# Two-layer trunk on one core: layers unrolled without barriers, a five-slot weight ring that keeps the low half in place, a new beginning, and weights split in halves of a tile

## The chip, the core and the metric

The kernel runs on one core of one Trainium2 chip. The metric is device time in microseconds (us), the lower the better. Five engines run their own instruction streams, tied together by semaphores only: PE (matmuls), DVE (vector), ACT (scalar, activations), POOL (GpSimd) and SP (SyncE, which here only issues DMAs and waits).

## The reference, cut to what matters

D = 1024, SEQ = 1024, batch 1, two layers, all float32:

```python
c_act = silu(c)
for l in range(2):
    sh_a, sc_a, ga_a, sh_m, sc_m, ga_m = split(c_act @ w_ada[l] + b_ada[l], 6)
    h = rmsnorm(x, g_mix[l]) * (1 + sc_a) + sh_a
    z = h @ w_in[l] + b_in[l]
    cb, cc, cu, q, kc, vc, ks, vs, kw, vw, nsa_g, merge_g = split(z)
    y_conv = short_conv(cb, cc, cu, conv_w[l]) @ w_up_conv[l]
    y_attn = nsa(rope(q), rope(kc), vc, rope(ks), vs, rope(kw), vw, nsa_g) @ w_up_attn[l]
    x = x + ga_a * ((sigmoid(g_c) * y_conv + sigmoid(g_a) * y_attn) @ w_o[l])
    h = rmsnorm(x, g_mlp[l]) * (1 + sc_m) + sh_m
    x = x + ga_m * (square(relu(h @ w_ff1[l])) @ w_ff2[l])
return rmsnorm(x, g_final)
```

`nsa` compresses kc and vc by a small MLP over blocks of 32 tokens and attends over the compressed blocks, over 8 selected blocks of 64 tokens, and over a window of 512.

## The kernel before, in words

**Layout.** Activations stand transposed in SBUF: `xT` is 8 chunks of 128 channels x 1024 tokens. A f32 product is three matmuls: both operands are split into a high part, rounded by writing it as fp32r (`hH`, `whi`), and a low part, the rest (`hL`, `wlo`); PE adds high·high, low·high and high·low (`dense`, L737 to L761). A weight tile is 128x1024 words (512 KB) and gives 8 x 3 products, each as a pair of matmuls of 512 columns: 48 matmuls.

**Weights.** `weight_plan` (L73) writes one layer's list of tiles: `split` (dense weights), `ada` (128 columns of `w_ada`, all 1024 rows) and `cmp` (a quarter of a compression weight). The first 32 dense tiles have an `ada` tile of this layer behind each, the first 16 `w_ff1` tiles one of the next layer (of layer 0's in the last layer, where nothing uses it). All go through a ring `wraw` of RAW = 3 slots in the list's order: SP (L670 to L698) loads tile n once the one three before it has let go, a `split` tile by `w_split` (POOL has split it), an `ada` tile by `ada_used` (DVE), a `cmp` tile by `cmp_used` (PE reads it directly, L813). POOL (L701 to L733) splits whole tiles into two slots of `whi` and `wlo`, L730 rounding and L732 subtracting, and waits there for the slot's last matmul (`lin_done`); PE waits for `w_split` once a tile. `ada_products` (L384) is a multiply of 1024 columns and a reduction on DVE, `ada_column` (L395) a matmul with a column of ones.

**Stages of a layer,** in PE's order: norm; conv branch (`cc`, `cu`, `cb` by 4); `gc`, `gc`, `uc` by 4 (a `uc` tile serves two short products); `ga`; `kc`, `vc`, `q0` to `q2`, compression of k, `q3`, compression of v, `ks`, `vs`, `kw`, `nsa`, `vw`, attention, `ua`, `wo`; norm; MLP (`f1`, `f2`). A norm: PE sums squares by 32 matmuls of one column (L406), DVE (L1283) and ACT make the reciprocal root, PE spreads it over `aux`, DVE multiplies chunk k (L1316), ACT writes `hH` (L1030), DVE `hL` (L1307). PE takes `cc0` and `cu0` side by side, chunk by chunk as `hL` comes.

**The beginning** (L410 to L579), a block of its own: DVE makes the rope tables, the x tiles are transposed (L506) as DVE works, ACT copies and squares, and DVE goes through the 16 `ada` tiles that the first norm needs, all through the ring of three. Then a block end, `clear()`, and the loop: `nc.Fori(0, DEPTH)` (L667) around one block, with `clear()` (L630) after each layer, where each engine clears a fifth of the semaphores between barriers. SP's first DMAs in a layer are three tiles, then `x_keep` (L680, all of `xT` to DRAM for the residual, 4 MB); DVE and ACT wait for it ahead of the conv branch, whose buffers lie over `xT`.

**The end** (L1644 to L1692): g_final on DVE and ACT, transposes back, outputs scaled and stored by token tile.

## Time and profile before

| | |
|---|---|
| three runs | 3528.22, 3532.52 (median), 3535.51 us |
| profiled execution: its own time, its span | 3531.86, 3530.1 us |
| PE busy, share of the span | 94% |
| DVE, POOL, ACT busy | 52%, 32%, 22% |
| DMA | 256.92 MB, mean 73 GB/s |

The span runs from the first to the last instruction; 1.8 us of the execution's time lie around it. PE is busy nearly throughout, so the time is PE's work plus the stretches in which it waits: these are read from the windows and from PE's waits by place. A matmul's "idle before" says how long PE stood still and which instruction released it.

### The profile page before, as it was taken

To read this page: it belongs to the slowest core of one execution; us is meant where nothing else is said; L and a number is where in the kernel's file an instruction comes from. 1 tells how busy PE (TensorE), PEld (TensorE's weight loads), DVE (VectorE), ACT (ScalarE), POOL (GpSimd) and SP (SyncE) were. 2 spreads that over 40 slices of the span, in tenths; PEclk is the share of its full clock that TensorE was granted. 3 is DMA by queue.
4 is the path that set the end of the run, shared out by engine and by line. 5 is a ranking of instruction groups with operands and counts; after the bars stand their busy time and mean duration, and the time that the engine had idled before them with its cause. 6 is when DMAs were issued, how large, how long until landed. Compare 5 with 4: busy or idle time off the path is not lost. (4 is left out here: it accounts for less than half of the span.)

```text
span 3530.1 us, 39234 instructions
## 1 busy us (share of the span) xinstructions
PE 3308.0 (94%) x15575; PEld 2687.7 (76%) x15605; DVE 1830.5 (52%) x1877; ACT 781.0 (22%) x1283; POOL 1119.9 (32%) x800
## 2 busy tenths in 40 slices
PE   4999999898898999999979999989979899999998
PEld 3788887676687888888868888767658788888887
DVE  7754344787636444333365443568865564433333
ACT  2100012666312000000120001147661210000002
POOL 3333322233332333333323333222333233333331
PEclk6999999999899999999989999999999999999999
DMA  5434431000422222111133343300005132211111
GB/s 166 147 96 131 138 96 48 1 1 1 157 66 66 72 72 68 52 48 48 36 122 96 113 137 111 81 7 1 1 9 195 37 96 72 72 48 48 48 48 60
DMA packets 349011, 256.92 MB, mean 73 GB/s; under 512 B 9500, under 2 KB 335506, under 8 KB 348563
## 3 DMA queue, kind: packets, MB, share of 16 engines
q1 hardware_dynamic: 334642, 209.75, 20.3%
q10 hardware_dynamic: 14177, 44.56, 3.4%
q8 instruction: 126, 2.06, 0.2%
q14 instruction: 66, 0.54, 0.0%
HBM read 223.87 MB, written 30.41 MB: 72 GB/s over the span
## 5 line engine op out<-in xcount | busy, mean ns | idle before, releaser
L730 POOL TENSOR_SCALAR whi<-wraw 128x1024 fp32r<-128x1024 f32 x238 | 266.2, 1119 | 1848.7 <-PE lin L759 1246.0
L759 PE MATMUL lin<-hH,whi 128*128 128x512 f32 x2272 | 719.1, 398 | 43.5 <-POOL wlo L732 35.4
L759 PE MATMUL lin<-hL,whi 128*128 128x512 f32 x2272 | 705.8, 392 | 0.0
L759 PE MATMUL lin<-hH,wlo 128*128 128x512 f32 x2272 | 705.2, 392 | 0.0
L732 POOL TENSOR_TENSOR wlo<-wraw,whi 128x1024 fp32r<-128x1024 f32 x238 | 644.2, 2707 | 19.9
L759 PEld LDWEIGHTS lin<-hH,whi 128*128 128x128 f32 x2272 | 423.9, 190 | 136.5 <-POOL wlo L732 39.5
L759 PEld LDWEIGHTS lin<-hL,whi 128*128 128x128 f32 x2272 | 430.5, 189 | 90.9
L759 PEld LDWEIGHTS lin<-hH,wlo 128*128 128x128 f32 x2272 | 429.9, 189 | 90.1
L1600 DVE SCALAR_TENSOR_TENSOR xT<-lin,adac,xT 128x1024 f32<-128x1024 f32 x144 | 184.8, 1283 | 542.3 <-PE lin L759 541.9
L711 POOL TENSOR_SCALAR prob<-prob,fac 128x640 f32<-128x640 f32 (+7 forms) x256 | 182.6, 713 | 471.2 <-DVE fac L1528 453.3
L759 PE MATMUL lin<-hidH,whi 128*128 128x512 f32 x1024 | 316.0, 390 | 0.0
L759 PE MATMUL lin<-hidL,whi 128*128 128x512 f32 x1024 | 315.5, 389 | 0.0
L759 PE MATMUL lin<-hidH,wlo 128*128 128x512 f32 x1024 | 315.5, 389 | 0.0
L1238 ACT ACTIVATE tmp<-lin 128x1024 f32<-128x1024 f32 x64 | 65.8, 1028 | 1077.6 <-PE lin L759 1076.5
L393 DVE TENSOR_REDUCE adared<-wraw 128x128 f32<-128x1024 f32 x112 | 223.3, 1993 | 94.8 <-PE pv L398 91.7
L1620 DVE TENSOR_TENSOR tmp<-tmp 128x1024 f32<-128x1024 f32 x64 | 84.0, 1313 | 352.0 <-ACT tmp L1238 352.0
L1544 DVE TENSOR_TENSOR pTL<-aux,pTH 128x512 fp32r<-128x512 f32 (+8 forms) x296 | 198.3, 686 | 50.9 <-ACT pTH L1188 49.4
L759 PEld LDWEIGHTS lin<-hidL,whi 128*128 128x128 f32 x1024 | 192.3, 188 | 39.9
L759 PEld LDWEIGHTS lin<-hidH,wlo 128*128 128x128 f32 x1024 | 192.3, 188 | 39.8
L759 PEld LDWEIGHTS lin<-hidH,whi 128*128 128x128 f32 x1024 | 191.8, 188 | 39.4
L388 DVE TENSOR_TENSOR wraw<-wraw,cT 128x1024 f32<-128x1024 f32 x112 | 201.2, 1796 | 27.3 <-DMA wraw<-in_w_ada 26.4
L1538 DVE TENSOR_REDUCE negm<-lin 128x1 f32<-128x640 f32 (+7 forms) x256 | 177.6, 703 | 37.3 <-PE lin L935 35.8
(233 smaller groups left out, 4025.5 us busy)
## 6 DMA issues: line engine op xcount, KB each, us to landing
wraw<-in_w_ff SPq DMA_DIRECT2D x128, 512.0 KB, 3.9
wraw<-in_w_ada SPq DMA_DIRECT2D x112, 512.0 KB, 4.8
wraw<-in_w_in SPq DMA_DIRECT2D x78, 512.0 KB, 3.8
x_keep<-xT SPq DMA_DIRECT2D x2, 4096.0 KB, 16.0
mix_keep<-tmp ACTq DMA_DIRECT2D x16, 512.0 KB, 2.6
gate_keep<-ropes ACTq DMA_DIRECT2D x16, 512.0 KB, 2.8
stG<-gate_keep ACTq DMA_DIRECT2D x16, 512.0 KB, 4.2
stM<-mix_keep ACTq DMA_DIRECT2D x16, 512.0 KB, 5.5
```

What stands on the lines that cost most here:

```text
L388: dve.tensor_tensor(w, w, cT[:, :].rearrange("p (k o) -> p k o", o=1).to_broadcast([P, KC, P]), ALU.mult).then_inc(ada_prod, 1)
L393: dve.tensor_reduce(adared[:, no % 2, :], w.rearrange("p k n -> p n k"), AX.X, ALU.add).then_inc(ada_used, 1)
L711: pool.tensor_scalar(p, p, fac[:, st["no"] % 2, i:i + 1], 1.0, ALU.mult, ALU.mult).then_inc(p_scaled, 1)
L730: pool.tensor_scalar(whi[:, s % SPL, :], wraw[:, n % RAW, :], 1.0, 1.0, ALU.mult, ALU.mult).then_inc(w_hi, 1)
L732: pool.tensor_tensor(wlo[:, s % SPL, :], wraw[:, n % RAW, :], whi[:, s % SPL, :].bitcast(F32), ALU.subtract).then_inc(w_split, 1)
L759: mm = pe.matmul(lin[c % 2][:, hf], w, m(k)[:, hf], start=first, stop=last)
L1238: act.activation(tmp[:, 0, :], slot(("f1", f))[:, :], ACT.Relu).then_inc(relu_made, 1)
L1538: dve.tensor_reduce(negm[:, m:m + 1], scores(u)[:, at:at + st["n"]], AX.X, ALU.max, negate=True).then_inc(max_made, 1)
L1544: dve.tensor_tensor(pt("low", x, r), turned(x, r), pt("high", x, r).bitcast(F32), ALU.subtract).then_inc(t_free[x["bank"]], 1)
L1600: dve.scalar_tensor_tensor(out=xT[:, i, :], in0=slot(name)[:, :], scalar=adac[:, gate + i:gate + i + 1], in1=xT[:, i, :], op0=ALU.mult, op ...
L1620: dve.tensor_tensor(tmp[:, 1, :], tmp[:, 0, :], tmp[:, 0, :], ALU.mult).then_inc(hid_sq, 1)
```

## The change

What it does:

- **No loop and no barriers.** The body is now `layer_programs(layer)` (after, L772), called for both layers; each engine runs beginning, layer 0, layer 1 and end in one block. `clear()` is gone; semaphores count on, or each layer has its own. A layer's first norm sums squares like the others.
- **Ring.** RAW = 5 slots. `wlo` is now `wraw` itself: POOL writes the low part over the raw tile, `whi` keeps its own two slots. A `split` tile's ring slot so comes free only with its last matmul (`lin_done`), and SP waits for that. Five slots of 4 KB and two of `whi` take the room of the former three and four (28 KB a partition both).
- **Halves.** POOL rounds and subtracts 512 columns at a time, with one `w_split` for each; PE waits ahead of k = 0 and of the middle k.
- **`w_ada` by rows.** A tile is 4 k-rows x 256 columns; DVE multiplies each row by its scalar of `cT` and adds, 4 instructions of 256 columns; two tiles make two column blocks. The 16 tiles that the last layer loaded for no use are gone.
- **Beginning.** x is transposed token tile by token tile and copied by DVE; ACT squares the token rows and sums them (`accum_out`); w_ada's first 2048 columns come as 16 DMAs of 512 KB with 2 KB runs, half 0 over `r_h` beside `xin`, half 1 in `r_m`; the norm's first four chunks wait for half 0 alone. The rope tables are made after `cb0`, in the conv branch. `x_keep` is two DMAs of 2 MB from ACT's queue. Layer 0's waits as before: ACT for its second half at the head of the conv branch (L1168), DVE as well (L1411).
- Next layer's `x_keep` is issued by ACT behind its squares (L1396); PE transposes the next layer's parameters in the sixth group of `f1` (L1146).

The diff's core:

```diff
-RAW = 3
+RAW = 5
...
-        (whi, wlo), (prob3,) = region("r_w", 2 * SPL * 1024, [(n, [P, SPL, 1024], F32R) for n in ("whi", "wlo")],
-                                      [("prob3", [P, HPG, SEQ], F32)])
+        (whi, wraw), (_, wlo), (prob3, pTH3, pTL3) = region(
+            "r_w", (SPL + RAW) * 1024,
+            [("whi", [P, SPL, 1024], F32R), ("wraw", [P, RAW, 1024], F32)],
+            [("whi_", [P, SPL, 1024], F32R), ("wlo", [P, RAW, 1024], F32R)],
...
 SP:
-                        if n >= RAW:
-                            o = n - RAW
-                            sp.wait_ge(dict(split=w_split, ada=ada_used, cmp=cmp_used)[TILES[o][0]], KIND_NO[o] + 1)
+                    if o is not None:
+                        if TILES[o][0] == "split":
+                            sp.wait_ge(lin_done, CHUNK[TILES[o][1], TILES[o][6][-1]] + 1)
+                        else:
+                            sp.wait_ge(dict(ada=ada_used, cmp=cmp_used)[TILES[o][0]], KIND_NO[o] + 1)
...
 POOL:
-                        pool.tensor_scalar(whi[:, s % SPL, :], wraw[:, n % RAW, :], 1.0, 1.0, ALU.mult, ALU.mult).then_inc(w_hi, 1)
-                        pool.wait_ge(w_hi, s + 1)
-                        pool.tensor_tensor(wlo[:, s % SPL, :], wraw[:, n % RAW, :], whi[:, s % SPL, :].bitcast(F32),
-                                           ALU.subtract).then_inc(w_split, 1)
+                    for i, hf in enumerate(half):
+                        raw, high = wraw[:, SLOT[n], hf], whi[:, s % SPL, hf]
+                        pool.tensor_scalar(high, raw, 1.0, 1.0, ALU.mult, ALU.mult).then_inc(w_hi, 1)
+                        pool.wait_ge(w_hi, 2 * s + i + 1)
+                        pool.tensor_tensor(wlo[:, SLOT[n], hf], raw, high.bitcast(F32), ALU.subtract).then_inc(w_split, 1)
...
 PE, dense:
-                            if j == 0:
-                                pe.wait_ge(w_split, SPLIT_NO[n] + 1)
+                            if j == 0 and k % (kk // 2) == 0:
+                                pe.wait_ge(w_split, 2 * s + k // (kk // 2) + 1)
...
 DVE, ada_products:
-            dve.tensor_tensor(w, w, cT[:, :].rearrange("p (k o) -> p k o", o=1).to_broadcast([P, KC, P]),
-                              ALU.mult).then_inc(ada_prod, 1)
-            dve.tensor_reduce(adared[:, no % 2, :], w.rearrange("p k n -> p n k"), AX.X, ALU.add).then_inc(ada_used, 1)
+            for i in range(ADA_K):
+                c = cT[:, ADA_K * t[3] + i:ADA_K * t[3] + i + 1]
+                if t[3] == 0 and i == 0:
+                    ins = dve.tensor_scalar(total, w[:, i, :], c, None, ALU.mult)
+                else:
+                    ins = dve.scalar_tensor_tensor(out=total, in0=w[:, i, :], scalar=c, in1=total, op0=ALU.mult, op1=ALU.add)
...
 begin_vector, after the copies of x:
+            ada(0, 0)
+            norm_diag(dve, 0)
+            for k in range(1, KC):
+                ada(0, k)
+            modulation(0)
+            dve.wait_ge(spread, 2)
+            norm_scaled(dve, 0, 0)
+            for k in range(1, 4):
+                norm_scaled(dve, 0, k)
+                norm_low(dve, 0, k - 1)
+                ada(1, k - 1)
+            norm_low(dve, 0, 3)
+            for k in range(3, KC):
+                ada(1, k)
+            modulation(1)
...
-            clear()
...
 scalar, head of a layer:
+                if layer:
+                    norm_root(act, n0)
...
+                else:
+                    keep_x(act, 0)
+                act.wait_ge(x_out[1], 16)
```

**POOL, one weight tile** (`lin_done` is PE's release of the slot, `raw_in` the tile's arrival, `w_hi` and `w_split` POOL's own steps). Before:

```order
L730 TENSOR_SCALAR whi<-wraw 128x1024 [waits lin_done,raw_in1,w_split]
L732 TENSOR_TENSOR wlo<-wraw,whi 128x1024 [waits w_hi]
```

and of the change:

```order
L867 TENSOR_SCALAR whi<-wraw 128x512 [waits lin_done,raw_in4,w_split]
L869 TENSOR_TENSOR wlo<-wraw,whi 128x512 [waits w_hi]
L867 TENSOR_SCALAR whi<-wraw 128x512
L869 TENSOR_TENSOR wlo<-wraw,whi 128x512 [waits w_hi]
```

Two instructions of 1024 columns become four of 512, in the order round, subtract, round, subtract, and the ring slot is written where it was read.

**SP, around the compression**, from the load of `q3` to that of `ks` (an ISA row at L698 is a wait carried by itself ahead of the DMA below it). Before:

```order
L698 ISA [waits cmp_used]
L698 DMA wraw<-in_w_in 128x8x128
L693 DMA wraw<-in_cmp_v_w 64x4x256 [waits cmp_used]
L693 DMA wraw<-in_cmp_v_w 64x4x256
L693 DMA wraw<-in_cmp_v_w 64x4x256 [waits cmp_used]
L693 DMA wraw<-in_cmp_v_w 64x4x256
L693 DMA wraw<-in_cmp_v_w 64x4x256 [waits w_split]
L693 DMA wraw<-in_cmp_v_w 64x4x256
L693 DMA wraw<-in_cmp_v_w 64x4x256 [waits cmp_used]
L693 DMA wraw<-in_cmp_v_w 64x4x256
L698 ISA [waits cmp_used]
L698 DMA wraw<-in_w_in 128x8x128
```

and of the change:

```order
L430 DMA wraw<-in_w_in 128x8x128 [waits lin_done]
L423 DMA wraw<-in_cmp_v_w 64x4x256 [waits cmp_used]
L423 DMA wraw<-in_cmp_v_w 64x4x256
L423 DMA wraw<-in_cmp_v_w 64x4x256 [waits cmp_used]
L423 DMA wraw<-in_cmp_v_w 64x4x256
L423 DMA wraw<-in_cmp_v_w 64x4x256 [waits cmp_used]
L423 DMA wraw<-in_cmp_v_w 64x4x256
L423 DMA wraw<-in_cmp_v_w 64x4x256 [waits cmp_used]
L423 DMA wraw<-in_cmp_v_w 64x4x256
L430 DMA wraw<-in_w_in 128x8x128 [waits lin_done]
L430 DMA wraw<-in_w_in 128x8x128 [waits cmp_used] x4
```

The first and the last-but-one load, `q3` and `ks`, now wait for `lin_done`, the end of an earlier tile's matmuls, and the eight loads of `cmp_v` stand behind the first of them.

**DVE, the beginning**, from the rope tables to the first `ada` tiles before (`adared`, `wraw`):

```order
L569 SCALAR_TENSOR_TENSOR nf<-nf 128x1024 [waits dve_p] x4
L572 TENSOR_SCALAR nf<-nf 128x1024 [waits dve_p]
L575 TENSOR_SCALAR nt<-nf 128x1024 [waits p_act]
L388 TENSOR_TENSOR wraw<-wraw,cT 128x1024 [waits raw_in0]
L393 TENSOR_REDUCE adared<-wraw 128x128 [waits ada_prod]
L388 TENSOR_TENSOR wraw<-wraw,cT 128x1024 [waits raw_in1]
```

and of the change, from the diagonal of the norm on (`acc` holds the sums over rows, `nt` a scaled chunk, `hL` its low part):

```order
L513 TENSOR_TENSOR tmp<-ident,rms 128x512
L715 SCALAR_TENSOR_TENSOR acc<-adar,cT,acc 128x1024 [waits adar0_in0]
L715 SCALAR_TENSOR_TENSOR acc<-adar,cT,acc 128x1024 [waits adar0_in1,dve_step] x2
L715 SCALAR_TENSOR_TENSOR acc<-adar,cT,acc 128x1024 [waits adar0_in2,dve_step] x2
L715 SCALAR_TENSOR_TENSOR acc<-adar,cT,acc 128x1024 [waits adar0_in3,dve_step] x2
L484 TENSOR_TENSOR adac<-pv,cols 128x4 [waits p_col]
L484 TENSOR_TENSOR adac<-pv,cols 128x4 [waits dve_step]
L489 SCALAR_TENSOR_TENSOR modA<-adac,cols 128x4 [waits dve_step]
L521 SCALAR_TENSOR_TENSOR nt<-xT,modA,aux 128x1024 [waits spread,p_vec]
L521 SCALAR_TENSOR_TENSOR nt<-xT,modA,aux 128x1024
L526 SCALAR_TENSOR_TENSOR hL<-nt,adac,hH 128x1024 [waits h_hi]
L713 TENSOR_SCALAR acc<-adar,cT 128x1024 [waits adar1_in0]
```

The rope work is no longer ahead of `w_ada`, the multiply and reduction of each column tile are one multiply-add for each k-row, and the first chunks' normalization stands ahead of the second half's sums.

## Rows read from the trace of the kernel before

**Rows 1.** The page, part 1: busy us, share of the span, instructions of each engine.

```profile
PE 3308.0 (94%) x15575; PEld 2687.7 (76%) x15605; DVE 1830.5 (52%) x1877; ACT 781.0 (22%) x1283; POOL 1119.9 (32%) x800
```

**Rows 2.** Table of stretches: length, busy us by engine (instructions), granted clock, DMA.

```profile
0.00:96.50 96.50, 38.94 (x141) 30.03 (x141) 71.83 (x58) 27.66 (x35) 34.50 (x72) 0.63 0.58 187
...
1106.50:1786.20 679.70, 679.65 (x3005) 563.33 (x3006) 279.50 (x162) 70.28 (x68) 239.77 (x122) 1.00 0.19 58
```

**Rows 3.** Timeline of the beginning: start, us, engine, line, operation, [idle before <-releaser].

```profile
14.34 3.67 PE L506 MATMUL lin<-ident,xin 128*128 128x128 f32 x16 [1.74 <-DMA xin<-in_x]
...
16.73 5.71 DVE L569 SCALAR_TENSOR_TENSOR nf<-nf 128x1024 f32<-128x1024 f32 x4
...
61.60 6.97 PE L406 MATMUL aux<-ones,tmp 128*128 128x1 f32 x32
...
96.49 1.19 PE L759 MATMUL lin<-hH,whi 128*128 128x512 f32 x2 [6.42 <-POOL wlo L732]
...
101.21 1.28 DVE L1307 SCALAR_TENSOR_TENSOR hL<-nt,adac,hH 128x1024 fp32r<-128x1024 f32 x1
...
101.33 1.15 ACT L1030 ACTIVATE hH<-nt,adac 128x1024 fp32r<-128x1024 f32 x1 [1.36 <-DVE nt L1316]
...
122.59 0.72 PE L759 MATMUL lin<-hH,whi 128*128 128x512 f32 x2 [2.24 <-POOL wlo L732]
```

**Rows 4.** DMA view of the first 20 us: GB/s in 40 slices of 0.5 us.

```profile
GB/s 0 0 0 8 8 172 238 377 418 442 393 385 410 393 426 434 393 434 410 418 442 385 401 411 403 411 339 329 304 285 298 293 297 286 291 292 290 159 19 0
```

**Rows 5.** The page, part 6: DMA issues, KB each, median us to landing.

```profile
wraw<-in_w_in SPq DMA_DIRECT2D x78, 512.0 KB, 3.8
x_keep<-xT SPq DMA_DIRECT2D x2, 4096.0 KB, 16.0
```

**Rows 6.** Stretches from the last pair before a norm to the next stage's first pair.

```profile
1064.35:1078.27 13.92, 7.57 (x38) 4.82 (x36) 6.82 (x9) 4.83 (x5) 3.39 (x2) 0.69 0.00 0
1786.44:1811.93 25.49, 9.16 (x39) 6.11 (x37) 10.99 (x15) 5.97 (x6) 7.62 (x4) 0.56 0.52 185
```

**Rows 7.** Timeline: the norm's first DVE instruction before the MLP and before layer 1.

```profile
1069.04 0.17 DVE L1283 TENSOR_SCALAR rms<-aux 128x8 f32<-128x8 f32 x1 [3.13 <-PE aux L406]
...
1798.60 0.17 DVE L1283 TENSOR_SCALAR rms<-aux 128x8 f32<-128x8 f32 x1 [10.28 <-issue]
```

**Rows 8.** Waits of PE from 110 to 500 us, then from 1815 to 2220 us.

```profile
PE lin L759 <- POOL wlo L732: 6.2, 5, 2.2
...
PE lin L759 <- POOL wlo L732: 6.5, 5, 2.2
```

**Rows 9.** Timeline: first pair of the third `w_ff1` tile, layers 0 and 1.

```profile
1106.55 0.79 PE L759 MATMUL lin<-hH,whi 128*128 128x512 f32 x2 [3.84 <-POOL wlo L732]
...
2821.90 1.22 PE L759 MATMUL lin<-hH,whi 128*128 128x512 f32 x2 [5.07 <-POOL wlo L732]
```

**Rows 10.** POOL by form: TENSOR_SCALAR of 512 columns (busy us, mean ns | idle before).

```profile
L711 POOL TENSOR_SCALAR prob<-prob,fac 128x512 f32<-128x512 f32 x32 | 22.6, 708 | 48.8 <-DVE fac L1528 46.5
```

**Rows 11.** Timeline, POOL's subtraction with DVE idle, and beside DVE's adds of two tensors.

```profile
88.94 2.34 POOL L732 TENSOR_TENSOR wlo<-wraw,whi 128x1024 fp32r<-128x1024 f32 x1
...
520.55 9.56 DVE L1415 TENSOR_TENSOR blk<-vcT,pe_cols 64x1008 f32<-64x1008 f32 x4
...
520.84 3.82 POOL L732 TENSOR_TENSOR wlo<-wraw,whi 128x1024 fp32r<-128x1024 f32 x1
```

**Rows 12.** Timeline: last quarter of the first compression, and the rotation behind `q3`.

```profile
517.72 2.05 PE L813 MATMUL pv<-blk,wraw 128*128 128x126 f32 x16 [2.01 <-DMA wraw<-in_cmp_k_w]
...
553.96 1.88 PE L790 MATMUL aux<-fbuf,rot 128*128 128x512 f32 x4
```

**Rows 13.** Line 398, matmuls: duration ns min/median/max.

```profile
L398 PE MATMUL pv<-ones,adared x224: 167/250/374, 30.1 to 3121.7; 128*128 128x1 f32 x112
```

**Rows 14.** Timeline of the end: last sum of squares, first scaled output.

```profile
3505.44 2.51 PE L406 MATMUL aux<-ones,tmp 128*128 128x1 f32 x16 [0.86 <-ACT tmp L1223]
...
3515.49 0.75 DVE L1684 TENSOR_SCALAR outb<-lin,rms 128x512 f32<-128x512 f32 x1
```

More of the change, by code:

```diff
@@ L76, in weight_plan @@
     tiles, chunk = [], {}
-    ada = iter(range(ADA_FIRST, NADA))
-    def dense(src, row, col, names, with_ada=False):
-        for n in names:
-            chunk[n] = len(chunk)
-        tiles.append(("split", src, row, col, 8 // len(names), names))
-        if with_ada:
-            tiles.append(("ada", next(ada)))
-    for j in range(CONV_W // P):
-        for name, off in (("cc", O_CC), ("cu", O_CU), ("cb", O_CB)):
-            dense("w_in", 0, off + P * j, [(name, j)], True)
-    for i in range(0, KC, 2):
-        dense("w_in", 0, O_MG + P * i, [("gc", i)], True)
-        dense("w_in", 0, O_MG + P * (i + 1), [("gc", i + 1)], True)
-        dense("w_up_conv", 0, P * i, [("uc", i), ("uc", i + 1)], True)
@@ L400, in sum_squares, with ada_column @@
+        def ada_column(pe, g, group):
+            pe.wait_ge(ada_used, ADA_TILES * (group + 1))
+            for i in range(2):
+                at = ADA_W // P * g + i
+                mm = pe.matmul(pv[:, 0, at:at + 1], adared[:, group % 2, i * P:(i + 1) * P], ones[:, 0:1], start=True, stop=True)
+            mm.then_inc(ada_mm, 1)
         def sum_squares(pe, first, last):
@@ new lines, in norm, with squares @@
+        def norm(dve, n, ready):
+            dve.wait_ge(ss_done, n)
+            dve.tensor_scalar(rms[:, :], aux[:, 0:NT], 1.0 / D, EPS, ALU.mult, ALU.add).then_inc(mean_made, 1)
+            norm_diag(dve, n)
+            ready()
+            dve.wait_ge(spread, 2 * (n + 1))
+            for k in range(KC):
+                norm_scaled(dve, n, k)
+                if k:
+                    norm_low(dve, n, k - 1)
+            norm_low(dve, n, KC - 1)
+        def squares(act, i, n, made):
+            act.wait_ge(x_made, made + i + 1)
+            if i >= 2:
+                act.wait_ge(ss_added, (n - 1) * (KC - 2) + i - 1)
+            act.activation(tmp[:, min(i, 1), :], xT[:, i, :], ACT.Square).then_inc(sq_made, 1)
@@ new lines, in scalar @@
+                if layer:
+                    fetch_tables()
+                for j in range(CONV_W // P):
+                    if j:
+                        freed(act, ("cu", j - 1))
+                    done(act, ("cc", j))
+                    act.activation(fbuf[:, 0, :], slot(("cc", j))[:, :], ACT.Identity,
+                                   bias=col(R_BIN + O_CC // P + j)).then_inc(free_sem(("cc", j)), 1)
+                    act.wait_ge(conv_made, v0 + j + 1)
+                    act.activation(cvH[:, j, :], ropes[:, 1, :], ACT.Copy).then_inc(cv_hi, 1)
+                    if layer == 0 and j == 0:
+                        rope_scalar(act)
+                    if layer == 0 and j == 1:
+                        act.wait_ge(rope_out, 32)
+                        fetch_tables()
@@ new lines, in vector @@
+                    done(dve, ("uc", i))
+                    if i >= 2:
+                        dve.wait_ge(mix_out[i % 2], 16 * (i // 2))
+                    dve.tensor_tensor(tmp[:, i % 2, :], slot(("uc", i))[:, :], fbuf[:, i % 2, :], ALU.mult).then_inc(free_sem(("uc", i)), 1)
+                    if i % 2:
+                        ada()
+                for i in range(KC):
+                    ada()
+                dve.wait_ge(ada_mm, layer * N_ADA + N_ADA - ADA_FIRST)
+                ada_part(dve, ADA_W // P * ADA_FIRST, NADA)
```

2286 lines of the change are left out of this document (1169 added, 1117 removed).

## The prediction

> **What bounds the kernel.** I read, in this order, the page's busy times, a table of stretches, PE's waits, and the timeline at the places where PE waits. PE is busy 3308.0 of 3530.1 us [rows 1]; from the MLP's third tile on it works 679.65 of 679.70 us at full clock [rows 2]. The change adds no matmul there, so it can win only where PE stands still. In the first 96.5 us PE does 38.94 us of work, none of it a dense product; `cb0`, behind the two products that wait for the norm, begins at 122.59 [rows 3]. The layer boundary takes 25.49 us where the same norm ahead of the MLP takes 13.92 [rows 6]. PE waits for POOL's split in the conv and `uc` stage, 6.2 us in layer 0 and 6.5 in layer 1 [rows 8], and at the third `w_ff1` tile, 3.84 and 5.07 us [rows 9]. The sum is made against the profiled execution, 3531.86 us; the median of the runs is 0.7 above that.
>
> **Beginning: −38 us.** Compared is the start of `cb0`, before 122.59 [rows 3]. The new chain, as times from the start:
> - x (4 MB) lands by about 13, at some 400 GB/s in the slices of [rows 4], and can be transposed from its first quarter on, near 7. 64 transposes at 3.67/16 = 0.23 us make 14.7 us, 8 copies on DVE at about 1.28 each less; so the copies are done at about 22 (20 to 25).
> - DVE then needs the parameters 1, `ada(0,0)` and the diagonal 2.3, seven multiply-adds of 1024 columns at 5.71/4 = 1.43 [rows 3], 10, columns and modulation 3 to 4, then two scaled chunks and a low part at 1.28: the first `hL` at 43. Three more chunks with a multiply-add of half 1 between take 4.0 each, five more multiply-adds 7, columns and modulation 4.5, and the last chunks 2.5 each, since ACT's 1.15 lies beside them: the eighth `hL` at about 75.
> - The data are no bound: by 400 GB/s half 0 of `w_ada` (4 MB) has landed near 24 and half 1 near 38.
> - PE does 6 pairs for each chunk of `cc0` and `cu0` beside that, and ends near 82: 2.7 us of the last chunk, and some backlog from chunks worked off at the low clock, at which a pair takes 1.19 in place of 0.79 or 0.72 [rows 3]; the positions' matmuls add 2.
> - `x_keep` is the other term. ACT issues it after its last `hH`, near 74; 4 MB took 16.0 us [rows 5], so the 2 MB that ACT and DVE wait for take about 8.5, and ACT drains `cc0` at about 83 to 84.
>
> So `cb0` starts at about 84.5, 38 us sooner; 30 to 41 by the ends above. The rope tables, ten DVE operations of 1.3 to 1.4 us, go beside the next two products, some 21 us, with 0 to 3 us to spare; ACT's sine work beside them too.
>
> **Boundary: −10.** Without block end, `clear()` and fetching the first tiles anew, the norm should look like the one ahead of the MLP: DVE's first instruction waits 3.13 us there, 10.28 here, with no releaser but issue [rows 7]. 25.49 − 13.92 = 11.6, less about 1.6 for the two `x_keep` issues and the root's table on ACT. Ends: 0 and −12.
>
> **Stalls in the mixed stages: −16.** Two tiles follow each other with little PE work between them (a `uc` product is half as long), and PE waits for load and split. With five slots the load is earlier, and the first half is ready after half a rounding, 0.71 [rows 10], and half a subtraction, 1.2 to 1.9 by 2.34 alone and 3.82 beside DVE [rows 11]: 2.0 in place of 3.5 to 4.9 us. Of 6.2 + 6.5 I take off 9.7, of 3.84 + 5.07 6.4. Ends: −10 and −19.
>
> **Compression and `ks`: +3.** Layer 0 waits 2.01 us for a quarter of `cmp_k` [rows 12], and nearly as long for one of `cmp_v`; with five slots both go, −4. In layer 1 the load of `q3` waits for the end of `q2`, and `cmp_v` stands behind it in SP's queue: nothing won. The load of `ks` now waits for `q3`'s last matmul, since the low half holds the slot: 3.8 landing [rows 5] and 2.0 for the first half, less the rotation's 1.88 [rows 12] and what is left: 3.5 us of new wait a layer, +7. Ends: −4 and +15.
>
> **The edits with one answer.** 16 fewer ada columns at 250 ns [rows 13], −4. The wait for each half inside a tile: 0, since POOL's four instructions take 4.0 to 4.6 us in all and PE's tile 10.9 (48 matmuls, 24 pairs at .45); they end long before PE comes to the tile. If that cover went, it would cost at most the second half's 2 us a tile. The `w_ada` products by rows: on DVE, beside PE; their cover is DVE's idle half. The end: first scaled output 7.5 us after the last sum of squares [rows 14], a block end among it; −5 (−3 to −6).
>
> **Sum:** −38 − 10 − 16 + 3 − 4 − 5 = −70, so 3462 for the profiled execution, and 3463 for the median. With the terms' ends, put together as independent, 3450 to 3476.
>
> **A rule beside a row.** POOL's subtraction took 2.34 us alone and 3.82 beside DVE's adds of two tensors [rows 11]. The Trainium skill, page "SBUF — State Buffer", section "SBUF: two separate sides", says that a DVE operation with two SBUF inputs and a GpSimd operation take one shared port pair, and that the one which comes second is blocked until the other's whole instruction is over. By that rule, four short POOL instructions can be blocked four times where two were blocked twice; the trace agrees that POOL is held up, by 1.5 us in this case.
>
> **Rivals.**
> - *Slower: the slot held by PE.* A ring slot is now occupied until the last matmul of its tile, and SP waits in order, so a late release holds up every load behind it. In some 80 tiles an `ada` tile stands between. If load and split came later than the tile is wanted, PE would wait in each. It decides from the point where load, queue and split take more than the lead of about two tile periods, 22 us; the rows give 3.8 to 4.8 landing, as much again queued, and 4 for the split, 13. It would have to cost 1 us in each of 80 tiles, +80, against the −70: 3542. Against it: there are 9 us to spare. 3%.
> - *Halves held twice.* Each of POOL's short instructions loses a DVE instruction's length, 1.28: first half ready after 2.0 + 2 × 1.28 = 4.6 us, so the mixed stages win only by the ring: −10 in place of −16, 3469. For it: 3.82 against 2.34. 15%. It is the rule of the Trainium skill named above, at work on halves.
> - *A slower beginning*: the sources of 2 KB runs at half the speed, or PE at the low clock through the first products, or the rope tables longer than their cover: +9, 3472. For it: the granted clock is 0.63 of full in the first 96.5 us [rows 2]. 15%.
> - *The boundary keeps its 25 us*: the 10.28 us by issue are not the barriers'. 3473. 5%.
> - *`ks` and the compression are worse*: each load that waits for `lin_done` finds PE waiting for it (landing, split, and `cmp_v` behind `q3`): +10, 3473. For it: the loads are in order in SP's queue. 10%.
> - *It does not do what it says*: the waits in the mixed stages come from DVE's or ACT's draining, not POOL, and stay: +14, 3477. Against it: the releaser named is `wlo` in each [rows 8, 9]. 7%.
> - *More*: beginning at its early end and no wait at `ks`: 3447. 5%.
>
> **How the numbers follow.** My forecast has the remaining 40%, 3463. 3442 to 3490 takes in all cases but the first, and two of them at once. A measurement can tell about 0.2%, 7 us, from no change. Faster by more than that: all cases but the slower one and a small part for several mishaps together, 95%; within 2%; slower 3%.
>
> **What would show it.** `cb0` starts at 82 to 88; the stretch from the last `f2` pair of layer 0 to the first pair of layer 1 is 13.5 to 16 us; PE's waits in the mixed stages fall to about 2 us in each layer, and to 1.3 at the third `w_ff1` tile; a wait of about 3.5 us stands ahead of `ks`; nothing in front of a tile's middle. Wrong would be: a wait by POOL inside tiles with an `ada` tile beside, an SP queue that waits for `lin_done` while PE waits for the next split, or a first dense product of layer 0 after 50 us.

## The result, and the profile after

The changed kernel takes 3470.4 us (median; 3469.55 to 3471.2), the kernel before 3532.89 beside it: a ratio of 0.9825, 95% interval 0.9808 to 0.9842. That is 62.5 us less. Forecast were 69.5 us less, 3463, with a range of 3442 to 3490. The profiled execution's span is 3468.6 us against 3530.1.

The page of the changed kernel: busy times, and two rows of the DMA issues.

```profile
PE 3288.9 (95%) x15541; PEld 2670.7 (77%) x15541; DVE 1591.7 (46%) x1998; ACT 771.2 (22%) x1274; POOL 1277.3 (37%) x1270
...
adar<-in_w_ada SPq DMA_DIRECT2D x16, 512.0 KB, 11.2
x_keep<-xT ACTq DMA_DIRECT2D x4, 2048.0 KB, 9.0
```

PE's busy time fell by 19.1 us [rows 1]; the other 42 us of the span's 61.5 are standing time that went. A half of `x_keep` lands after 9.0 us (8.5 were reckoned), a row block of the new `w_ada` loads, eight of them queued, after 11.2.

Where they went is read by stretches between instructions of PE that both kernels have. The ends are starts of instructions in the two timelines; the forecast's terms stand beside.

| stretch | before | after | difference | forecast |
|---|---|---|---|---|
| start to `cb0` | 122.59 | 88.29 | −34.3 | −38 |
| `cb0` to compression k, layer 0 | 387.60 | 381.84 | −5.8 | |
| compression k to `ua0`, layer 0 | 421.10 | 428.78 | +7.7 | |
| first MLP pair to third `w_ff1` tile, layer 0 | 28.28 | 24.98 | −3.3 | |
| third `w_ff1` tile to the boundary's sum | 679.89 | 678.84 | −1.1 | |
| boundary | 25.49 | 14.78 | −10.7 | −10 |
| first pair of layer 1 to compression k | 413.11 | 407.56 | −5.6 | |
| compression k to `ua0`, layer 1 | 421.44 | 427.08 | +5.6 | |
| first MLP pair to third `w_ff1` tile, layer 1 | 29.01 | 24.95 | −4.1 | |
| third `w_ff1` tile to the last sum | 680.84 | 674.68 | −6.2 | |
| last sum (its first part) to the end | 27.36 | 23.34 | −4.0 | −5 |
| `ua`, `wo`, norm ahead of the MLP, both layers | 293.39 | 293.48 | +0.1 | 0 |
| mixed stages together | | | −18.7 | −16 |
| compression and `ks` together | | | +13.3 | +3 |
| the MLPs behind the third tile together | | | −7.2 | −4 (ada columns) |
| all | 3530.1 | 3468.6 | −61.5 | −70 |

The stages of a layer need one correction to the list above: around the compressions, PE's order in both kernels is `q0`, `q1`, compression of k, `q2`, compression of v, `q3`, `ks`. The other order, `q2` ahead of compression k and `q3` ahead of compression v, is that of the weight list, in which the tiles are loaded. The column "before" is one execution. e8 below runs the same code there with more barriers, and its stretches differ by up to 3.4 us (first pair of layer 1 to compression k 416.48 for 413.11); by it the mixed stages would come to −24.8 and the compression and `ks` to +17.5. Those of the changed kernel repeat better: `cb0` to compression k is 381.84 there and in e2, 381.85 in e1.

Two terms missed. The beginning, timeline of the changed kernel (start, us, engine, line, operation, idle before and its releaser):

```profile
41.53 1.28 DVE L526 SCALAR_TENSOR_TENSOR hL<-nt,adac,hH 128x1024 fp32r<-128x1024 f32 x1
...
58.75 3.58 PE L655 MATMUL pv<-ones,acc 128*128 128x1 f32 x16 [21.33 <-DVE acc L715]
...
62.19 1.20 PE L894 MATMUL lin<-hH,whi 128*128 128x512 f32 x2
...
70.78 0.84 ACTq L391 DMA_DIRECT2D x_keep<-xT  x2
...
77.12 0.35 DVE L445 TENSOR_SCALAR adared<-wraw,cT 128x256 f32<-128x256 f32 x1 [3.88 <-DMA x_keep<-xT]
...
86.38 1.98 PE L664 MATMUL aux<-posf,ones 1*128 1x512 f32 x4
...
88.29 0.73 PE L894 MATMUL lin<-hH,whi 128*128 128x512 f32 x2
```

The first low part is made by 42.8 (41.53 and 1.28), as forecast with 43. But PE's first dense pair starts only at 62.19: in PE's own queue the column sums of half 1 (L655, at 58.75) stand ahead of it, and they wait 21.33 us for DVE. So the head start of the first four chunks is not used by PE, and its 48 pairs end just ahead of the positions' matmuls at 86.38. `x_keep` had landed by 77.12, where DVE goes on, 9 us before PE was done. `cb0`, at 88.29, is just past the 82 to 88 that the forecast gave as its sign. [rows 3] has the same place before.

Waits of PE in the changed kernel (what waits <- for whom: us in total, times, the longest):

```profile
PE pv L655 <- DVE acc L715: 28.9, 2, 21.3
...
PE lin L894 <- POOL wlo L869: 10.6, 5, 3.9
...
PE pv L943 <- DMA wraw<-in_cmp_v_w: 8.1, 2, 4.0
```

The splits that came late cost 35.4 us in 14 waits before and 10.6 in 5 now, and PE waits 8.1 us for `cmp_v`, where before it waited 3.9 for `cmp_v` and 3.8 for `cmp_k`. Between 85 and 480 us there is no such wait any more, where [rows 8] had 6.2. The wait for `cmp_v` and the one for the split of `ks` lie here:

```profile
488.40 0.38 SPq L430 DMA_DIRECT2D wraw<-in_w_in  x1
...
488.82 5.21 SPq L423 DMA_DIRECT2D wraw<-in_cmp_v_w  x8
...
494.71 10.10 PE L943 MATMUL pv<-blk,wraw 128*128 128x126 f32 x64 [4.05 <-DMA wraw<-in_cmp_v_w]
...
515.76 5.42 SPq L430 DMA_DIRECT2D wraw<-in_w_in  x5
...
519.60 0.85 POOL L867 TENSOR_SCALAR whi<-wraw 128x512 fp32r<-128x512 f32 x1 [22.38 <-issue]
...
521.94 1.19 PE L894 MATMUL lin<-hH,whi 128*128 128x512 f32 x2 [3.89 <-POOL wlo L869]
```

SP could load `q3` (488.40) only when `q2`'s last matmul had let its slot go, and the loads of `cmp_v` stand behind it (488.82); PE has waited 4.05 us when it begins compression v. In the same way `ks` is loaded only at 515.76, when `q3`'s last matmul is done; POOL begins to split it at 519.60, and PE starts it at 521.94 after a wait of 3.89. Layer 1 has the same two waits, 4.02 and 3.89. Table of stretches (length; busy by engine; at the end granted clock, DMA share, GB/s): beginning, boundary, compression v, `ks`, and the first 4 us of `ks` alone.

```profile
0.00:96.50 96.50, 55.89 (x240) 44.73 (x241) 67.56 (x71) 21.86 (x29) 29.96 (x78) 0.79 0.63 224
1749.50:1764.28 14.78, 8.31 (x37) 5.66 (x36) 6.93 (x9) 3.55 (x4) 3.73 (x4) 0.74 0.79 319
494.71:504.56 9.85, 9.85 (x64) 9.85 (x65) 3.41 (x2) 0.06 (x1) 2.42 (x2) 0.71 0.63 128
521.94:536.95 15.01, 15.01 (x53) 11.64 (x53) 4.94 (x4) 1.52 (x3) 8.93 (x8) 0.81 0.32 77
...
521.94:526.00 4.06, 4.06 (x10) 3.19 (x11) 3.71 (x4) 0.47 (x2) 3.89 (x3) 0.50 1.16 281
```

In the beginning PE now does 55.89 us of work in 96.5 at a clock of 0.79, before 38.94 at 0.63 [rows 2], and the boundary is 14.78 us long where [rows 6] has 25.49. The clock column has what the forecast left out: 0.71 in compression v and 0.81 in `ks`, of 1.00. In `q3`, ahead of the wait, it was 1.00 (504.56 to 518.05); in the first 4.06 us of `ks` it is 0.50, the low level, 1.2 GHz of 2.4. So the work behind these waits is slower as well. The shorter waits of the kernel before, 2.01 and 1.88 us inside the two compressions of layer 0, did not do that: from 542.96 to 557.00, in `q3` behind them, its clock was 1.00. The rows at the third `w_ff1` tile and at the end answer to [rows 9, 14]. From the start of the last sum's second part to the first scaled output it is 4.47 us now (3452.43 less 3447.96), and was 10.05; the forecast's 7.5 counts from the sum's end, and from there it is 2.3. Behind that output the end takes 1.6 us longer than before (16.2 for 14.6), which is why the whole stretch gives 4.0 and not 5.6:

```profile
1070.66 0.70 PE L894 MATMUL lin<-hH,whi 128*128 128x512 f32 x2 [0.95 <-POOL wlo L869]
...
3447.96 2.18 PE L467 MATMUL aux<-ones,tmp 128*128 128x1 f32 x16 [0.86 <-ACT tmp L546]
...
3452.43 0.75 DVE L1769 TENSOR_SCALAR outb<-lin,rms 128x512 f32<-128x512 f32 x1
```

### The profile page after: what moved, and what is told of

Read it like the earlier page. It is cut to its first block, busy times and chain, and to the rows that moved or that the text cites. A ratio compares the mean times of both kernels' runs of the same rounds, so it can differ in the third digit from the quotient of the medians.

```text
span 3468.6 us, 38561 instructions
## 1 busy us (share of the span) xinstructions
PE 3288.9 (95%) x15541; PEld 2670.7 (77%) x15541; DVE 1591.7 (46%) x1998; ACT 771.2 (22%) x1274; POOL 1277.3 (37%) x1270
## 4 chain that ended last, share of the span: by engine, by line
PE 86%; DVE 8%; issue 3%; ACT 2%; POOL 1%; DMA 0%; SPq 0%; POOLq 0%; ACTq 0%; DVEq 0%
PE lin L894 74%; PE aux L1086 2%; DVE pTL L1632 2%; PE pv L1100 2%; DVE negm L1626 1%; PE pv L1101 1%; PE lin L1062 1%; PE lin L1063 1%; PE lin L1041 1%; ACT pTH L1333 1%; PE pv L943 1%; DVE acc L715 1%; PE aux L920 0%; PE lin L1065 0%; DVE tmp L1652 0%
## 5 line engine op out<-in xcount | busy, mean ns | idle before, releaser
L867 POOL TENSOR_SCALAR whi<-wraw 128x512 fp32r<-128x512 f32 x476 | 379.8, 798 | 1637.7 <-PE lin L894 1510.4
L869 POOL TENSOR_TENSOR wlo<-wraw,whi 128x512 fp32r<-128x512 f32 x476 | 710.1, 1492 | 39.7
L1701 DVE TENSOR_TENSOR tmp<-tmp 128x1024 f32<-128x1024 f32 x64 | 137.8, 2154 | 440.0 <-ACT tmp L1379 439.8
L447 DVE SCALAR_TENSOR_TENSOR adared<-wraw,cT,adared 128x256 f32<-128x256 f32 x280 | 194.4, 694 | 9.4
L1333 ACT ACTIVATE pTH<-aux 128x512 fp32r<-128x512 f32 (+8 forms) x296 | 173.2, 595 | 105.5 <-PE aux L1086 79.8
L1317 ACT ACTIVATE prob<-lin,negm 128x640 f32<-128x640 f32 (+7 forms) x256 | 178.4, 697 | 81.7 <-DVE negm L1626 80.6
## 6 DMA issues: line engine op xcount, KB each, us to landing
adar<-in_w_ada SPq DMA_DIRECT2D x16, 512.0 KB, 11.2
```

The source lines that it names most:

```text
L447: ins = dve.scalar_tensor_tensor(out=total, in0=w[:, i, :], scalar=c, in1=total, op0=ALU.mult, op1=ALU.add)
L867: pool.tensor_scalar(high, raw, 1.0, 1.0, ALU.mult, ALU.mult).then_inc(w_hi, 1)
L869: pool.tensor_tensor(wlo[:, SLOT[n], hf], raw, high.bitcast(F32), ALU.subtract).then_inc(w_split, 1)
L1317: act.activation(prob_of(no, i)[:, 0:st["n"]], scores(u)[:, at:at + st["n"]], ACT.Exp, bias=negm[:, m:m + 1], accum_out=sums[:, m:m + 1]). ...
L1333: act.activation(pt("high", x, r), turned(x, r), ACT.Copy).then_inc(t_hi, 1)
L1701: dve.tensor_tensor(tmp[:, 1, :], tmp[:, 0, :], tmp[:, 0, :], ALU.mult).then_inc(hid_sq, 1)
```

## The experiments

All are compared with the kernel before that ran beside them, and with the changed kernel by its span of 3468.6 us. e1 to e4 ran on one chip; there e3, which turned out to change nothing, is the measure for the other three: 3471.2. e5 to e8 ran on a second chip and e9 to e11 on a third; the kernel before took 3536.5, 3535.9 and 3535.4 us on the three.

**e1: the list in the order of use.**

```diff
-        ... ("q1", O_Q + P), ("q2", O_Q + 2 * P)):
+        ... ("q1", O_Q + P)):
...
-        dense("w_in", 0, O_Q + 3 * P, ["q3"])
+        dense("w_in", 0, O_Q + 2 * P, ["q2"])
         tiles += [("cmp", layer, 1, t) for t in range(CMP_T)]
-        for name, off in (("ks", O_KS), ...
+        for name, off in (("q3", O_Q + 3 * P), ("ks", O_KS), ...
```

> The changed kernel with the weight tiles listed, loaded and split in the order in which PE takes them: q1, the four quarters of cmp_k, q2, the four of cmp_v, q3, ks, where the change lists q2, cmp_k, q3, cmp_v, ks. Theory A (the ring slot that is held until the last matmul, with SP waiting in order, makes the new waits ahead of compression v and of ks, 4.0 and 3.9 us in each layer, and the low granted clock after them the rest): both waits go, the stretch from compression k to vs is some 6 us shorter a layer than in the changed kernel, 3468.6 becomes about 3456, median 3457 to 3460. Theory B (the waits are those of the split in halves, POOL late or blocked by DVE there): the waits stay, and the time within 2 us of the changed kernel's 3470.

Measured: 3446.1 us (3444.74 to 3447.01), ratio 0.9746 [0.9729, 0.9762], span 3444.2: 24.4 us less than the changed kernel, twice what was expected. Both waits are gone, for `q2` is loaded at 468.51, before compression k, and `cmp_v` from 472.01 on:

```profile
468.51 0.38 SPq L430 DMA_DIRECT2D wraw<-in_w_in  x1
...
472.01 1.26 SPq L423 DMA_DIRECT2D wraw<-in_cmp_v_w  x2
```

and the same two stages, compression v and `ks`, as stretches:

```profile
491.27:498.40 7.13, 7.13 (x64) 7.13 (x65) 4.64 (x3) 2.11 (x2) 5.99 (x5) 1.00 0.60 155
511.83:524.17 12.34, 12.34 (x54) 9.70 (x53) 6.78 (x6) 3.43 (x4) 2.67 (x4) 1.00 0.08 23
```

They run at a clock of 1.00, 7.13 us in place of 9.85 and 12.34 in place of 15.01. Theory A holds, with a size too small: it expected 6 us a layer, and from compression k to `ua0` e1 is 13.5 and 11.8 us shorter, the waits and what PE loses behind them together. It is the best single edit of the study.

**e2: half 1's column sums ahead of chunk 4.**

```diff
-            for h in range(2):
-                begin_columns(pe, h)
+            begin_columns(pe, 0)
...
+                def first(k):
+                    if layer == 0 and k == 4:
+                        begin_columns(pe, 1)
+                    pe.wait_ge(h_lo, 2 * layer * KC + k + 1)
```

> The changed kernel with the column sums of half 1 taken out of PE's beginning and put ahead of chunk 4 of the first dense pair. Theory A (PE stands in its own queue behind these sums from 42.8 us, when the first low part is there, to 62.2): PE begins dense work near 43, cb0 starts at 78 to 80 in place of 88.3, so 9 us less: about 3461. Rival B (PE falls behind at the low clock, so the column sums come late and with them chunks 4 to 7): 3 us less or nothing, 3467 to 3471. Rival C (x_keep's landing at about 77 and ACT behind it hold cb0 at 84 or later): about 3466.

Timeline of PE:

```profile
42.78 1.22 PE L893 MATMUL lin<-hH,whi 128*128 128x512 f32 x2 [5.45 <-DVE hL L526]
...
58.66 2.92 PE L654 MATMUL pv<-ones,acc 128*128 128x1 f32 x16 [3.27 <-DVE acc L714]
...
78.94 1.98 PE L663 MATMUL aux<-posf,ones 1*128 1x512 f32 x4
80.85 0.73 PE L893 MATMUL lin<-hH,whi 128*128 128x512 f32 x2
```

Dense work begins at 42.78, the sums are where they were (58.66), and `cb0` starts at 80.85, 7.4 us sooner. So A, and not C: `x_keep` did not hold it. The four executions took 3461.34 to 3469.82 us, median 3466.2, ratio 0.9805 [0.9789, 0.9821]. They fell in two groups, 3461.3 and 3462.6 against 3469.7 and 3469.8 (mean clock 0.976 and 0.973); the profiled one is of the first. Only half of them kept the 8 us. What the others lost has no trace, and stays open.

**e3: `x_keep` issued after the fourth high part.**

```diff
                 for k in range(4 * h, 4 * h + 4):
                     norm_high(act, 0, k)
+                if h == 0:
+                    keep_x(act, 0)
...
-                    keep_x(act, 0)
```

> The changed kernel with layer 0's x_keep issued by ACT after the fourth high part, at about 52 us, in place of the eighth, 70.8. Theory A (cb0 is held by PE, which ends its first two products at 86.3, and not by x_keep): no change, 3470 within 1 us, cb0 still at 88. Rival B, my prediction's reading (x_keep's landing and ACT's copy behind it are as late as PE): 1 to 3 us less, 3467 to 3469.

3471.2 us (3469.85 to 3472.01), ratio 0.9817, span 3469.3: no change. `x_keep` does not limit, neither here nor, by e10, behind the earlier PE of e2.

**e4: whole-tile splits again.**

```diff
-                    for i, hf in enumerate(half):
-                        raw, high = wraw[:, SLOT[n], hf], whi[:, s % SPL, hf]
+                    raw, high = wraw[:, SLOT[n], :], whi[:, s % SPL, :]
...
-                            if j == 0 and k % (kk // 2) == 0:
-                                pe.wait_ge(w_split, 2 * s + k // (kk // 2) + 1)
+                            if j == 0 and k == 0:
+                                pe.wait_ge(w_split, s + 1)
```

> The changed kernel with POOL rounding and subtracting whole tiles again and PE waiting once a tile; all else as changed. Theory A (the halves make the first half ready 1.6 us sooner wherever the split is the last to come): waits 1.6 longer at ks in each layer and at the third w_ff1 tile (0.95 becomes 2.5), perhaps 1 us in the uc stages: 6 to 8 us more, 3476 to 3478. Rival B (the ring of five does it all, halves are for nothing, since each short POOL instruction is held up by DVE): within 2 us of 3470. Rival C (the halves cost something, DVE's operations slowed beside POOL): 3465 to 3468.

3487.5 us (3487.19 to 3488.08), ratio 0.9863 [0.9847, 0.988]: 16 us more than e3 beside it, twice what A expected. Taken out last, the halves are worth a quarter of the whole change. `cb0` to compression k stays near 382 us with whole tiles (472.67 less 89.19 is 383.5), so most of that stage's gain of 5.8 is there without them; the halves pay at the third `w_ff1` tile (3.39 us of wait, timeline below, against 0.95), at `ks` (18.85 us from `q3` on, against 17.38), in the MLP behind it, and at the first tiles. PE's waits for the split are 20.5 us in 6, against 10.6 in 5.

```profile
1076.31 3.27 POOL L868 TENSOR_TENSOR wlo<-wraw,whi 128x1024 fp32r<-128x1024 f32 x1
...
1077.41 3.26 DVE L1703 TENSOR_TENSOR hidL<-tmp,hidH 128x1024 fp32r<-128x1024 f32 x1
...
1079.73 0.83 PE L893 MATMUL lin<-hH,whi 128*128 128x512 f32 x2 [3.39 <-POOL wlo L868]
```

**e5: PE kept at work in its two waits.**

```diff
+                def idle_work():
+                    for _ in range(16):
+                        pe.matmul(pv[:, 1, 384:512], ident[:, :], ident[:, :], start=True, stop=True)
...
+                idle_work()
                 compress(1)
...
+                idle_work()
                 dense("ks", H, L)
```

> The changed kernel with 16 matmuls of 128 columns (identity times identity, into an unused part of pv, read by nobody) ahead of compression v and 16 ahead of ks, so that PE works through most of its two waits there. Theory A (a new wait costs its own length and then what PE loses at the low clock behind it): the loads are no sooner, so compression v and ks begin where they did, within 0.5 us, but compression v takes 7.1 us and not 9.9 or 8.8, and ks to vs 12.4 and not 15; 8 to 10 us less in all, about 3461. Rival B (the slow matmuls behind the waits are slow for another reason, say late quarters of cmp_v or POOL's second half): no change or up to 2 us more, 3470 to 3473.

3464.0 us (3461.73 to 3465.14), ratio 0.9796 [0.978, 0.9813], span 3461.4: 7.2 us less, although the two stages start where they did (494.88 and 520.59 against 494.71 and 521.94, the second sooner by what compression v saved). Stretches of compression v and `ks`:

```profile
494.88:503.23 8.35, 7.93 (x64) 7.36 (x65) 3.56 (x2) 0.00 (x0) 2.41 (x2) 1.00 0.72 149
520.59:532.87 12.28, 12.28 (x53) 9.68 (x53) 4.96 (x4) 1.51 (x3) 8.95 (x8) 1.00 0.40 97
```

PE's idle time right ahead of compression v is 0.59 us in place of 4.05. The clock is 1.00 in both. `ks` takes 12.28 us, as in e1; compression v 8.35, not 7.1, since its later quarters arrive one by one (7.93 of 8.35 busy). So useless matmuls made the kernel faster: A holds, a little under its 8 to 10. Of e1's 24.4 us, 7.2 are what the clock alone gives back while the loads stay late. The four waits, 15.9 us less 1.4 that e1 keeps, make 14.5 by my reckoning; the last 2.7 no run separates, late quarters among them.

**e6: halves, but one wait at the tile's head.**

```diff
-                            if j == 0 and k % (kk // 2) == 0:
-                                pe.wait_ge(w_split, 2 * s + k // (kk // 2) + 1)
+                            if j == 0 and k == 0:
+                                pe.wait_ge(w_split, 2 * s + 2)
```

> The changed kernel with POOL still splitting in halves but PE waiting for both halves at the head of a tile. Theory A (whole-tile split costs 17 us because a late split makes PE wait longer and then run at the low clock, and half of that is the wait for the second half): every late split about 2 us later, at ks, at the third w_ff1 tile and in the first pairs after the norms, some 10 to 17 us more, 3480 to 3487, as with whole tiles. Rival B (the gain of halves lies in shorter POOL instructions, which hold up DVE less): within 3 us of 3470.

3494.6 us (3491.96 to 3495.38), ratio 0.9884 [0.9868, 0.9901]: 24 us more than the changed kernel and 7 more than whole tiles. PE's waits for the split:

```profile
PE lin L894 <- POOL wlo L869: 26.6, 6, 6.7
```

26.6 us against 10.6, and against 20.5 with whole tiles (e4). At the third `w_ff1` tile PE waits 4.70 us, in e4 3.39. Rival B is out: four short instructions are not better than two long ones, they are later; all of the gain, and more, lies in PE's beginning on the first half.

**e7: the kernel before with halves.** The same edit as the change's in POOL and `dense`, with SP waiting for `w_split` twice as high; ring of three, own low slots.

> The kernel before, its ring of three and separate low parts kept, with the split in halves and a wait for each. Theory A (halves help wherever the split comes last, whatever the ring): the five stalls of each layer, cb0 and the third w_ff1 tile 1.5 us shorter each or gone, 12 to 18 us less than before, 0.995 to 0.9965 of it. Rival B (the ring's depth did it, the load being the late part in a ring of three): 0 to 5 us less.

3515.6 us (3512.8 to 3518.5), ratio 0.9946 [0.9929, 0.9962], span 3511.0: 20 us less than the 3535.9 beside it, 19 by the spans, so just beyond A's upper end. `cb0` and the third `w_ff1` tile:

```profile
120.28 0.70 PE L761 MATMUL lin<-hH,whi 128*128 128x512 f32 x2 [1.16 <-POOL wlo L734]
...
1096.86 1.13 PE L761 MATMUL lin<-hH,whi 128*128 128x512 f32 x2 [3.66 <-POOL wlo L734]
```

`cb0` to compression k is 381.7 us here, as in the changed kernel, with the ring of three. In layer 1 the same place (first pair to compression k) takes 409.4 here and 408.2 in e4, for 413.1 before and 407.6 with both. So for the conv and `uc` stage either cure does most of it, halves or ring, and they don't add. At the third `w_ff1` tile neither does it alone: the wait is 3.66 and 2.23 us in the two layers here, 3.39 and 3.32 in e4, and 0.95 in both with halves and ring together. The boundary is 22.35 us here, so 3.1 of its 25.49 were a late split.

**e8: the kernel before with each clearing done twice.**

```diff
         clear()
+        clear()
```

> The kernel before with every clearing of the semaphores and its barriers done twice. It prices one such block. Theory A (block end and clearing make the difference between the boundary's 25.5 us and the other norm's 13.9): 3 to 4 us more each time, at the beginning, at the boundary and at the end, 9 to 12 us in all. Rival B (clearing is cheap, and the boundary's time is code fetch or the ring's refill): under 3 us in all.

3545.0 us (3540.81 to 3548.06), ratio 1.0021 [1.0011, 1.0031]: 9.1 us more, inside A's 9 to 12. They are not even: 2.7 at the start (`cb0` at 125.24), 2.8 at the end (30.17 from the last sum to the end, against 27.36), 6.7 at the boundary (32.14 in place of 25.49; the medians say a little less than the three together):

```profile
1790.90:1823.04 32.14, 8.36 (x39) 5.42 (x37) 14.35 (x17) 6.93 (x7) 7.73 (x4) 0.62 0.42 150
```

This prices one more of them, not the one that was removed; the removal itself gave 10.7 at the boundary, where the block end and the ring's refill go too, and no run separates these. The profiled execution's span is 14.8 us longer, 2.7 more than the three places: among them the third `w_ff1` tile of layer 0, whose wait is 5.07 us here and 3.84 before, with the same code.

**e9 and e10: both edits, and `x_keep` with them.** e9 is e1 and e2 together, e10 adds e3.

> The changed kernel with both edits, the weight list in the order of use and half 1's column sums ahead of chunk 4. Theory: they are in different stages, so they add: 24.3 and 4 to 7.7 us less than the changed kernel's 3470.4, about 3439, in two groups of executions 8 us apart if the second edit does again what it did alone (3461 to 3462 and 3470). Rival: the earlier start of dense work is given back at the low clock in each execution, 3445.

> The same with x_keep issued after the fourth high part too. Theory (with PE done at about 79, x_keep's landing near 77 and ACT's copy of cc0 behind it are just in time): 0 to 1 us less than the kernel with two edits. Rival: x_keep in the middle of the norm delays ACT's high parts by its 0.8 us of issuing: 1 us more.

e9: 3438.9 us (3438.52 to 3440.25, five executions), ratio 0.9726 [0.9713, 0.974], span 3437.0. The two edits add, and there is one group of executions, not two. e10: 3439.8 (3438.84 to 3441.32), the same within the measurement. e9 is the best kernel of the study, 31.5 us below the changed one: it gains 96.6 us on the 3535.4 beside it, against 62.5.

**e11: the order of use with whole tiles.** e1 and e4 together.

> The changed kernel with the list in the order of use and whole-tile splits. Theory (of the 17 us that whole-tile splits cost, those around compression and ks go where no load is late any more; the rest, at the first tiles of each stage and the third w_ff1 tile, stay): 12 us more than the list in the order of use with halves, 3458. Rival (halves matter only where a load is late): 3448 or less.

3462.1 us (3459.28 to 3464.52), ratio 0.9791 [0.9776, 0.9806]: 16 us more than e1. Nothing of the 16 went with the late loads. Compression k to `ks` is the same in both (41.80 and 41.79 us); the difference lies from `ks` to `ua0` (377.33 against 373.49 in layer 0, 375.04 and 373.54 in layer 1), in the MLPs (707.25 and 703.20 against 703.77 and 699.90), at the first tiles of the layers and from layer 1's start to compression k (409.66 against 407.53). The expectation's direction held, its split of the sum didn't.

## Why the prediction was right, and where it was off

It was right in sign and size, 7 us short. But two terms missed by 3.7 and 10.3 us, and two gave 2.7 and 3.2 back, so the number is nearer than its parts, which is luck. Two of the three things that it named as signs of being wrong came to pass: the first dense product of layer 0 begins at 62.19, not before 50, and SP waits for `lin_done` while PE waits for the next tiles, ahead of compression v and of `ks`. The range was put too low from its own ends: their middles are −35.5, −6, −14.5, +5.5, −4.5 and the columns' −4, −59 together, so that put together as independent they give 3460 to 3487 and not 3450 to 3476.

- **Beginning,** −38, measured −34.3. The chain on DVE was right to a microsecond: first low part at 43, measured 42.8; the eighth at 75, measured 73.3 (the last two start at 70.66 and take 2.59). Wrong was the step "PE does 6 pairs for each chunk beside that, and ends near 82": it took PE to be free. I had the column sums in DVE's account and not in PE's queue; e2 takes them out of the way and gets 7.4 us. With PE free, as the forecast took it, PE ends 6.4 us behind the last low part (72.50 to 78.94), near the 7 reckoned; in the changed kernel it ends 13.1 us behind it (73.25 to 86.38). That the last low part came 1.7 us sooner than forecast hid some of this. The forecast's other term, ACT draining `cc0` at 83 to 84 behind `x_keep`, does not hold either: `x_keep` had landed by 77.12, and e3, which issues it sooner, changes nothing.
- **Boundary,** −10, measured −10.7; the norm takes 14.78 against 14.10 ahead of the MLP. e8 shows that one more clearing there costs 6.7 by itself, and e7 that 3.1 were a late split, which halves alone cure; the forecast had counted the whole to barriers and refill. The rival that the 25 us stay is out.
- **Mixed stages,** −16, measured −18.7. The size is right, the account was not: I gave the ring and the halves each a share of each stall. By e4 and e7 the conv and `uc` stage is mostly cured by either alone, and the third tile only by both together.
- **Compression and `ks`,** +3, measured +13.3. The wait ahead of `ks` was forecast at 3.5 and is 3.89. For `cmp_v` the forecast was that layer 0 gains 2 and layer 1 nothing, since its loads stand behind `q3`'s; it did not carry that through: `q3`'s load itself starts only when `q2` is done, and compression v is the very next thing on PE, so 4.05 us of wait take the place of 1.88, and in layer 1 4.02 of 1.98. Compression k gained in both layers, 2.3 and 2.0 us, where the forecast had 2 in layer 0 alone. And no wait had a price for the clock behind it: e5 measures that alone at 7.2 us for four waits, e1 the whole at 24.4. The rival "`ks` and the compression are worse, +10" is what happened, and its 3473 is nearer than 3463.
- **Ada columns,** −4. The MLPs behind the third tile gained 7.2, but not by the columns alone: with whole tiles (e4) the same two stretches are 680.40 and 676.24 us, against 679.89 and 680.84 before, 4.1 less together; the other 3.1 come with the halves. So the term fits, and the halves' share in the MLP was not seen.
- **End,** −5, measured −4.0: the first scaled output came 5.6 us sooner, but what is behind it took 1.6 longer, for which no run shows a cause.
- **"The wait for each half inside a tile: 0."** Right; the PE waits that are left are at heads of tiles. But the price of the halves was never written down as a term by itself. It is the largest single one after the beginning, 16 us by e4 and 20 by e7.
- **The slower rival,** the slot held by PE, decides at 22 us and does not occur beside the `ada` tiles. Where it bites is elsewhere: where several tiles are used up between two dense products, so that the slot five back is that of the tile still at work.
- **Halves held twice.** Half right. The first half, which PE waits for, is not held: at the third `w_ff1` tile it took 0.62 and 1.27 us (last rows below), 1.97 from the start of the one to the end of the other, as the sum had it. The second half is: 1.59 and 2.14 us. It costs nothing only because PE is at work on the first; e6, where PE waits for both, is 7 us slower than whole tiles.
- **Not isolated.** The deeper ring and the low half kept in the ring's slot were never run apart, nor was the unrolling or `w_ada` by rows taken out alone.

## To carry to other kernels

Where a slot comes free only with its last use and the queue that refills it is in order, list the loads in the exact order of use: one tile too early in the list holds up all behind it, and e1 got 24 us for moving two entries. Halves pay by the consumer's beginning on the first, not by their shortness (e4, e6). Price each wait of PE twice, once for its length and once for the slower work behind it. Before a head start on one engine is counted, read the queue of the engine that shall use it: what stands ahead there, and for whom it waits.
